# The first block's last norm as one combined sum with the recurrent layer's norm, and recurrent operands in PSUM

## The chip, the cores and the metric

The kernel runs on one core of a Trainium2 chip. The metric is the device time of one execution in microseconds (us), the median of several runs. Engines: TensorE (PE) with its weight load (PEld), VectorE (DVE), ScalarE (ACT), GpSimd (POOL), SyncE (SP, here only DMA issues).

## What is computed

A sequence of 512 tokens of width 1024 goes through a first block (modulated attention with a gated linear branch, then a convolutional feed-forward) and a second block of four layers, each a mixer and an MLP. Layers 0 and 3 have the recurrent mixer, layer 1 a spatial one, layer 2 a short convolution. What matters here, with `rms_norm(x, g) = x * rsqrt(mean(x*x) + EPS) * g` and EPS 1e-6:

```python
# end of the first block
x_lat = x_lat + gt2 * conv_ffn(h, ...)
return rms_norm(x_lat, final_g)

# start of the second block, layer 0 (recurrent) and layer 3 (recurrent)
h = _rmsnorm(x, norm_mix_g[i])
gate, xr = split(h @ w_in, 2)
gate = gelu(gate)
xr = causal_dwconv(xr, conv_w) + conv_b            # 4 taps
r  = sigmoid(block_diagonal(xr, gate_a_w) + gate_a_b)
ig = sigmoid(block_diagonal(xr, gate_x_w) + gate_x_b)
log_a = -8 * r * softplus(-lam)
a = exp(log_a)
u = sqrt(-expm1(2 * log_a)) * (ig * xr)
hs = scan(a, u)                                    # over time
x = x + (hs * gate) @ w_out
```

Two norms stand back to back where the blocks meet: the first block's last, of the sum x, and the recurrent layer's, of the normalised x. The normalised x is itself needed later, for the residual.

## The kernel before, in words

**Layout.** Everything is kept transposed: features on the 128 partitions, the 512 tokens along the free axis, so x is 8 tiles `x[:, k, :]` of 128x512 and a recurrent width of 1280 is 10 tiles. Each product is made in three parts for precision: an operand is split into a high and a low half (`h_hi`, `h_lo`; `rec_hi`, `rec_lo`), the weights too (`w_hi`, `w_lo`), and a tile of product is high by high, low by high, high by low (L1540 to L1551).

**Weights.** SP loads panels of 8 weight tiles into a ring of 4 slots, in order of use. GpSimd makes `w_hi` (L1473) and then `w_lo` (L1483) of each; it goes on when TensorE has begun with the panel that frees the slot. All are chained by semaphores (`panel_made`, `panel_used`).

**TensorE** writes outputs in a fixed order, output number o into bank o mod 4 of `acc` (4 PSUM banks); `begin_out` waits until the output four before has been taken. `stat` is a fifth bank, `side` three more. Norm sums are a product of `ones` with a sum of squares (L1583).

**The handover between the blocks.** VectorE adds each output of the last down projection to x (`gated_add`, L1350); ScalarE squares it (`sq`, L805); VectorE adds up the squares (`add_up`, L1069). When all 8 are in, TensorE sums over partitions (L1583), ScalarE takes the root (L815), VectorE the reciprocal (L1075) and rescales x by it and by `final1` (L1428). Each rescaled tile goes through `feed` and `feed_low`: square and high half on ScalarE (L1699, L1703), sum and `h_lo` on VectorE (L1885 or L1888, L1895). TensorE's first projection waits for `h_lo` tile by tile; its norm sum, root (L1709) and reciprocal (L1900) follow. The projections run on unnormalised h, and the outputs are rescaled by `rstd` afterwards.

**The recurrent layer** (functions `recurrent` on PE at L1588, on ACT at L1711, on DVE at L1915) has two halves of five tiles. TensorE makes five projections, then for each tile two gate products of two or three weight tiles each; a product for tile m needs neighbouring tiles of `rec_hi` and `rec_lo` (`BD`). After both halves come ten more projections (the y phase) and the down projection, whose first four outputs are made in two passes over the ten inputs (`down_in_two`).

VectorE's order is written out by hand: `convolved` rescales the bank (L1923), writes the bias into the first three columns (L1931, from `ones` in SBUF), and adds the four taps (L1936, two of L1939, and L1942, which writes into the bank). ScalarE (`conv_high`, L1719 and L1720) copies the bank to `rec_x` and to `rec_hi`; VectorE's `low` (L1948) makes `rec_lo` from the bank and sets the bank free. In the first half the order is convolved(m), low(m-1); in the second half the five ratios of the first half (L1963, on `rec_u` and `rec_sq`, both in SBUF) stand behind the first convolution. ScalarE's `decays` (L1730) makes tanh and two exponentials per tile, waiting for a ratio before it reuses one of the four tiles of `rec_sq`; `roots` (L1749) follow. In the y phase VectorE multiplies and scans the second half (`scanned`, L1966), and per output rescales the bank, multiplies it with the scan (`gated`, L1980) after ScalarE's gelu, and makes `y_low`. In the order before, y outputs 2 and on stand behind all five scans.

## Time and profile before

| | |
|---|---|
| median of 3 runs | 3293.4 us (3291.03 to 3296.08) |
| the profiled execution's own time | 3291.95 us |
| its span in the profile | 3290.2 us |
| mean granted TensorE clock | 0.972 of full speed |
| busy share PE, DVE, ACT, POOL | 95%, 46%, 21%, 57% |
| HBM traffic | 302.84 MB read, 93 GB/s over the span |

The profile is one execution taken by the hardware profiler. Its times are in us from the start of the span. The ends of the pipelined matmuls are modelled, so two starts in a row tell more than one duration. In a row such as `acc<-h_hi,w_hi` the output stands left of the arrow and the inputs right; the names in an overlay carry its prefix (`rec_rec_lo` is `rec_lo`). A row "A <- B" of the waits says that A's engine stood idle until B's instruction released it. A line number is that of the program text above.

The handover lies near 1086 to 1118 us, the first recurrent layer from there to about 1290, the second from about 2705 to 2890.

### The profile page before, as it was taken

The page shows a single profiled execution, that of the slowest core. Times are in us where ns is not written, and L with a number is a line of the kernel's source. Part 1 is how long each engine was busy: PE and PEld are TensorE (multiplying, and loading weights), DVE is VectorE, ACT ScalarE, POOL GpSimd, SP SyncE. Part 2 cuts the span into 40 slices and gives each one's busy share as a digit, 9 for nine tenths or more (in the row PEclk, how much of TensorE's full clock was granted, in tenths as well). Part 3 has the DMA queues.
Part 4 walks back from the last instruction along what each step waited for, and adds up shares of the span by engine and source line. Part 5 has one row for each costly group of instructions (what it writes and reads, how often), then busy time and mean ns, then how long its engine had stood idle before and what let it go on. Part 6 is the DMA issues. An engine that isn't in the chain of part 4 may idle for free.

```text
span 3290.2 us, 37587 instructions
## 1 busy us (share of the span) xinstructions
PE 3116.0 (95%) x13568; PEld 2492.1 (76%) x13568; DVE 1528.4 (46%) x1918; ACT 707.3 (21%) x1203; POOL 1876.1 (57%) x1030
## 2 busy tenths in 40 slices
PE   5878799989999799999999999999999998999998
PEld 3666646868888578888878888888888886888886
DVE  7876763247633774422236422266522247642222
ACT  3244463111100352200013211110211114421110
POOL 3412203646666466666666666666666665666664
PEclk8988899999999899999999999999999999999999
DMA  6601002222222122222222222222222222222221
GB/s 245 244 26 39 33 1 77 96 77 96 96 96 96 59 95 96 95 97 96 96 96 90 96 96 96 96 96 96 91 98 97 97 91 89 93 93 97 97 95 69
DMA packets 86009, 306.68 MB, mean 93 GB/s; under 512 B 9552, under 2 KB 10064, under 8 KB 85632
## 3 DMA queue, kind: packets, MB, share of 16 engines
q1 hardware_dynamic: 82512, 297.73, 26.6%
q10 hardware_dynamic: 3376, 7.24, 0.6%
q8 instruction: 87, 1.43, 0.2%
q14 instruction: 34, 0.28, 0.0%
HBM read 302.84 MB, written 2.10 MB: 93 GB/s over the span
## 4 chain that ended last, share of the span: by engine, by line
PE 83%; DVE 11%; ACT 2%; issue 2%; SPq 1%; DMA 1%; ACTq 0%; DVEq 0%
PE acc L1520 78%; PE side L727 1%; DVE rec_rec_x L1939 1%; DVE ada_more L1105 1%; PE acc L705 1%; DVE state L1251 1%; DMA xc<-in_ctx 1%; SPq L497 1%; DVE rec_rec_u L1963 0%; PE acc L631 0%; DVE acc L1942 0%; DVE rec_rec_x L1936 0%; DVE square_sum L1888 0%; DVE acc L1923 0%; DVE rec_rec_x L1931 0%
## 5 line engine op out<-in xcount | busy, mean ns | idle before, releaser
L1483 POOL TENSOR_TENSOR w_lo<-w_raw,w_hi 128x1024 fp32r<-128x1024 f32 x513 | 1243.6, 2424 | 1345.3 <-PE acc L1520 1298.9
L1520 PE MATMUL acc<-h_hi,w_hi 128*128 128x512 f32 x2224 | 881.6, 396 | 61.9 <-DVE state L1251 14.5
L1520 PE MATMUL acc<-h_hi,w_lo 128*128 128x512 f32 x2224 | 872.4, 392 | 0.0
L1520 PE MATMUL acc<-h_lo,w_hi 128*128 128x512 f32 x2224 | 872.4, 392 | 0.0
L1473 POOL TENSOR_SCALAR w_hi<-w_raw 128x1024 fp32r<-128x1024 f32 x513 | 650.1, 1267 | 37.3 <-DMA w_raw<-in_weights 37.3
L1520 PEld LDWEIGHTS acc<-h_hi,w_hi 128*128 128x128 f32 x2224 | 420.9, 189 | 170.1 <-issue 18.8
L1520 PEld LDWEIGHTS acc<-h_hi,w_lo 128*128 128x128 f32 x2224 | 421.3, 189 | 86.4
L1520 PEld LDWEIGHTS acc<-h_lo,w_hi 128*128 128x128 f32 x2224 | 421.6, 190 | 85.3 <-issue 1.7
L1906 DVE TENSOR_TENSOR x<-acc,x 128x512 f32 (+1 forms) x160 | 110.7, 692 | 635.5 <-PE acc L1520 635.3
L1520 PE MATMUL acc<-mlp_hid_hi,w_hi 128*128 128x512 f32 x1024 | 403.5, 394 | 0.0
L1520 PE MATMUL acc<-mlp_hid_hi,w_lo 128*128 128x512 f32 x1024 | 401.4, 392 | 0.0
L1520 PE MATMUL acc<-mlp_hid_lo,w_hi 128*128 128x512 f32 x1024 | 397.4, 388 | 0.0
L1834 ACT ACTIVATE mlp_hidden<-mlp_relu 128x512 f32<-128x512 f32 x128 | 81.0, 633 | 884.1 <-DVE mlp_relu L2115 884.1
L1913 DVE TENSOR_TENSOR mlp_hid_lo<-mlp_hidden,mlp_hid_hi 128x512 f32 (+1 forms) x128 | 157.4, 1230 | 177.5 <-ACT mlp_hid_hi L1835 177.5
L1520 PEld LDWEIGHTS acc<-mlp_hid_hi,w_lo 128*128 128x128 f32 x1024 | 192.2, 188 | 45.1
L1520 PEld LDWEIGHTS acc<-mlp_hid_lo,w_hi 128*128 128x128 f32 x1024 | 192.2, 188 | 43.0
L1520 PEld LDWEIGHTS acc<-mlp_hid_hi,w_hi 128*128 128x128 f32 x1024 | 192.5, 188 | 38.4
L2115 DVE SCALAR_TENSOR_TENSOR mlp_relu<-acc,rstd 128x512 f32<-128x512 f32 x128 | 88.6, 692 | 268.7 <-PE acc L1520 267.7
L1699 ACT ACTIVATE side<-x 128x512 f32<-128x512 f32 x72 | 43.4, 602 | 468.9 <-DVE x L1906 458.8
L1520 PE MATMUL acc<-rec_rec_hi,w_hi 128*128 128x512 f32 x264 | 107.8, 408 | 22.4 <-DVE rec_rec_lo L1948 22.4
L1383 DVE SCALAR_TENSOR_TENSOR ff_conv<-acc,table,ff_conv 128x441 f32<-128x441 f32 (+2 forms) x176 | 122.4, 695 | 6.3
L1520 PE MATMUL acc<-rec_rec_hi,w_lo 128*128 128x512 f32 x264 | 106.5, 403 | 0.0
(323 smaller groups left out, 3505.2 us busy)
## 6 DMA issues: line engine op xcount, KB each, us to landing
w_raw<-in_weights SPq DMA_DIRECT2D x513, 512.0 KB, 3.2
ada<-in_ada SPq DMA_DIRECT2D x36, 512.0 KB, 5.4
ada_more<-in_ada SPq DMA_DIRECT2D x10, 512.0 KB, 18.4
x<-in_x ACTq DMA_DIRECT2D x16, 256.0 KB, 6.6
out<-x SPq DMA_DIRECT2D x8, 256.0 KB, 2.2
cvec<-in_cvec ACTq DMA_DIRECT2D x1, 1024.0 KB, 5.8
ada_n<-in_ada SPq DMA_DIRECT2D x2, 512.0 KB, 17.5
xc<-in_ctx SPq DMA_DIRECT2D x1, 1024.0 KB, 16.9
```

What stands on the lines that cost most here:

```text
L497: sp.dma_start(ada_slot[slot], io["ada"][m]).then_inc(ada_in[slot], 16)
L705: pe.matmul(out[:, 0:c1 - c0], q_t[0:QK, h, P * qb:P * qb + P], k_t[0:QK, h, c0:c1], start=True, stop=True).then_inc(out_made, 1)
L727: ins = pe.matmul(side[rows, h % 2, :], v_mla[:, b, 64 * h:64 * h + 64], p_t[:, b, :], start=(b == 0), stop=(b == KB - 1))
L1383: ins = dve.scalar_tensor_tensor(out=out, in0=src[:, r0 + r:r1 + r, c0 + c:c1 + c], scalar=col("conv_w", FF1 * tap + j), in1=out, op0=ALU. ...
L1473: pool.tensor_scalar(w_hi[:, slot, :], w_raw[:, slot, :], 1.0, 1.0, ALU.mult, ALU.mult).then_inc(hi_made, 1)
L1483: pool.tensor_tensor(w_lo[:, slot, :], w_raw[:, slot, :], w_hi[:, slot, :].bitcast(F32), ALU.subtract).then_inc(panel_made, 1)
L1520: ins = pe.matmul(out, lhs, rhs, start=start, stop=stop, skip_group_check=group)
L1699: act.activation(squares(norm, k), x[:, k, :], ACT.Square).then_inc(squared, 1)
L1834: act.activation(M["hidden"][:, o % 4, :], M["relu"][:, o % 4, :], ACT.Square)
L1906: dve.tensor_tensor(tile, bank(o), tile, ALU.add).then_inc(out_taken[o % BANKS], 1)
L1913: dve.tensor_tensor(lo, whole_, hi.bitcast(F32), ALU.subtract).then_inc(made_sem, 1)
L2115: dve.scalar_tensor_tensor(out=M["relu"][:, o % 4, :], in0=bank(o), scalar=0.0, in1=rstd[:, :], op0=ALU.max, op1=ALU.mult).then_inc(out_ta ...
```

## The change

1. The first block's last norm is no longer made ahead of the recurrent layer. `FIRST_NORMS` goes from 4 to 3, `norm_sum(3)` is gone. Behind each `gated_add` ScalarE makes two squares, of x times `final1` and of x alone, and the high half of x times the product of both gains (`gain2[:, KT:]`); VectorE (`both_sums`) adds up the first squares, adds EPS times the second ones to it, keeps a sum of the second ones alone, and makes `h_lo` directly from x. The combined root uses `eps_eps`, EPS squared.
2. x itself is normalised later: TensorE makes a second sum product behind the norm's (L1583 stays), ScalarE its root, and VectorE (`first_norm`) a reciprocal and eight rescalings of x, inside the y phase's loop of the first recurrent layer.
3. `convolved` accumulates all four taps in `rec_x`, the newest tap first over all 512 columns, and the bias operation on three columns is gone. `conv_high` copies `rec_x` back into the bank and makes `rec_hi` from `rec_x`.
4. The exponential that the ratio reads goes to PSUM (`side` and `stat`) for four of five tiles, and ScalarE's wait for a ratio is gone. In the second half ratios 3 and 4 stand behind the second convolution.
5. In the y phase outputs 2 and 3 are moved in between the scans, and from output 4 on the bank of the next output is rescaled, not that of the one after.

```diff
-FIRST_NORMS = 4
+FIRST_NORMS = 3
...
-rec_a=([P, RT, T], F32), rec_u=([P, HALF, T], F32), rec_sq=([P, 4, T], F32))
+rec_a=([P, RT, T], F32), rec_u=([P, HALF, T], F32), rec_sq=([P, T], F32))
...
+        def decay_square():
+            return scan_input()[0:4] + [M["rec_sq"][:, :]]
...
             down(2)
-            norm_sum(3)
...
             for k in range(KT):
                 wait_taken(act, o + k)
-                sq(k, 3, x)
-            root_of(3)
-            for k in range(KT):
-                feed(k, NORM0, ("norm_mix", 0), lambda k: act.wait_ge(x_normed, k + 1), o)
+                act.wait_ge(summed, KT * NORM0 + k - 1)
+                act.activation(spare_bank[k % 2], x[:, k, :], ACT.Square, scale=col("final1", k)).then_inc(squared, 1)
+                if k:
+                    act.wait_ge(own_summed, k)
+                act.activation(side[:, 0, :], x[:, k, :], ACT.Square).then_inc(own_squared, 1)
...
+                act.activation(h_hi[:, k, :], x[:, k, :], ACT.Copy, scale=gain2[:, KT + k:KT + k + 1]).then_inc(h_hi_made, 1)
...
+            def both_sums(k):
+                scaled_sum, own_sum, own_square = square_sum[:, :], square[:, 0, :], side[:, 0, :]
+                dve.wait_ge(squared, KT * NORM0 + k + 1)
...
+                    link(dve.tensor_tensor(scaled_sum, spare_bank[k % 2], scaled_sum, ALU.add))
+                dve.wait_ge(own_squared, k + 1)
+                own(dve.scalar_tensor_tensor(out=scaled_sum, in0=own_square, scalar=EPS, in1=scaled_sum, op0=ALU.mult, op1=ALU.add),
+                    summed, KT * NORM0 + k + 1)
...
+                    own(dve.tensor_tensor(own_sum, own_square, own_sum, ALU.add), own_summed, k + 1)
+                dve.wait_ge(h_hi_made, KT * NORM0 + k + 1)
+                dve.scalar_tensor_tensor(out=h_lo[:, k, :], in0=x[:, k, :], scalar=gain2[:, KT + k:KT + k + 1],
+                                         in1=h_hi[:, k, :].bitcast(F32), op0=ALU.mult, op1=ALU.subtract).then_inc(h_lo_made, 1)
...
                             norm_sum(norm)
+                            if inst == 0:
+                                pe.wait_ge(own_summed, KT)
+                                pe.matmul(side[:, 0, :], ones[:, :], square[:, 0, :], start=True, stop=True).then_inc(own_stat, 1)
...
-                    act.activation(M["rec_x"][:, m, :], bank(o), ACT.Copy)
-                    act.activation(M["rec_hi"][:, m, :], bank(o), ACT.Copy).then_inc(rec_hi_made, 1)
+                    act.activation(bank(o), M["rec_x"][:, m, :], ACT.Copy)
+                    act.activation(M["rec_hi"][:, m, :], M["rec_x"][:, m, :], ACT.Copy).then_inc(rec_hi_made, 1)
...
-                            if i >= 4:
-                                act.wait_ge(rec_ratio, done + i - 3)
...
-                            act.activation(M["rec_sq"][:, i % 4, :], a, ACT.Exp, scale=rec_cl[:, 0, m:m + 1]).then_inc(rec_tanh, 1)
+                            act.activation(decay_square()[i], a, ACT.Exp, scale=rec_cl[:, 0, m:m + 1]).then_inc(rec_tanh, 1)
...
+                if inst == 0:
+                    act.wait_ge(own_stat, 1)
+                    act.activation(square[:, 1, :], side[:, 0, :], ACT.Sqrt, bias=col("eps"), scale=1.0 / D).then_inc(own_root, 1)
+                    act.wait_ge(own_root, 1)
...
-                    dve.tensor_scalar(acc_[:, 0:A_TAPS - 1], ones[:, 0:A_TAPS - 1], col("a_conv_b", first + m), None, ALU.mult)
-                    for j in range(A_TAPS - 1):
...
+                    for back in range(A_TAPS):
+                        tap = w[A_TAPS - 1 - back]
+                        dve.wait_ge(rec_tap, n0 + back + 1)
+                        if back == 0:
+                            dve.tensor_scalar(acc_, xr, tap, col("a_conv_b", first + m), ALU.mult, ALU.add).then_inc(rec_tap, 1)
+                        else:
+                            dve.scalar_tensor_tensor(out=acc_[:, back:], in0=xr[:, 0:T - back], scalar=tap, in1=acc_[:, back:],
+                                                     op0=ALU.mult, op1=ALU.add)\
+                               .then_inc(rec_conv if back == A_TAPS - 1 else rec_tap, 1)
...
+                def first_norm(i):
+                    if i == 0:
+                        dve.wait_ge(own_root, 1)
+                        dve.reciprocal(square[:, 1, :], square[:, 1, :]).then_inc(own_rstd, 1)
+                        dve.wait_ge(own_rstd, 1)
+                    for k in range(2 * i - 2, 2 * i):
+                        if 0 <= k < KT:
+                            dve.scalar_tensor_tensor(out=x[:, k, :], in0=x[:, k, :], scalar=col("final1", k), in1=square[:, 1, :],
+                                                     op0=ALU.mult, op1=ALU.mult).then_inc(x_normed, 1)
...
                 convolved(o, HALF)
-                for i in range(HALF):
+                for i in range(3):
                     ratio(first, i)
                 conv_low(o, HALF)
+                convolved(o + 1, HALF + 1)
+                for i in range(3, HALF):
+                    ratio(first, i)
+                conv_low(o + 1, HALF + 1)
...
-                for i in range(2, HALF):
-                    scanned(first + HALF, i, gates[1])
-                for m in range(2, RT):
+                scanned(first + HALF, 2, gates[1])
+                gated(o + 2, 2)
+                scanned(first + HALF, 3, gates[1])
+                y_low(o + 2, 2)
+                scaled_bank(o + 4, rec_gated)
+                gated(o + 3, 3)
+                scanned(first + HALF, 4, gates[1])
+                y_low(o + 3, 3)
+                for m in range(4, RT):
+                    if m + 1 < RT:
+                        scaled_bank(o + m + 1, rec_gated)
                     gated(o + m, m)
-                    if m + 2 < RT:
-                        scaled_bank(o + m + 2, rec_gated)
                     y_low(o + m, m)
+                    if inst == 0:
+                        first_norm(m - 4)
```

## Rows read from the trace of the kernel before

**Rows 1.** The page, busy time of each engine, whole span.

```profile
PE 3116.0 (95%) x13568; PEld 2492.1 (76%) x13568; DVE 1528.4 (46%) x1918; ACT 707.3 (21%) x1203; POOL 1876.1 (57%) x1030
```

**Rows 2.** TensorE's waits, whole span: who for, us in total, times, longest.

```profile
PE acc L1520 <- DVE rec_rec_lo L1948: 26.2, 10, 3.8
...
PE acc L1520 <- DVE h_lo L1895: 11.7, 8, 7.1
```

**Rows 3.** Timeline of the handover: start, us, engine, operation, [idle before it <- releaser].

```profile
1083.28 1.05 POOL L1473 TENSOR_SCALAR w_hi<-w_raw 128x1024 fp32r<-128x1024 f32 x1
...
1086.09 0.75 DVE L1350 SCALAR_TENSOR_TENSOR x<-acc,mod,x 128x512 f32<-128x512 f32 x1 [2.73 <-PE acc L1520]
...
1091.25 3.36 DVE L1075 RECIPROCAL side<-root 128x512 f32<-128x512 f32 x1 [2.89 <-ACT root L815]
...
1098.55 2.35 POOL L1483 TENSOR_TENSOR w_lo<-w_raw,w_hi 128x1024 fp32r<-128x1024 f32 x1 [14.23 <-PE acc L1520]
...
1098.65 2.80 DVE L1895 SCALAR_TENSOR_TENSOR h_lo<-x,table,h_hi 128x512 fp32r<-128x512 f32 x1
...
1112.36 0.50 PE L1520 MATMUL acc<-h_hi,w_hi 128*128 128x512 f32 x1 [0.30 <-DVE h_lo L1895]
```

**Rows 4.** Waits in the recurrent layers: first layer three, second layer two.

```profile
1142.51 0.50 PE L1520 MATMUL acc<-rec_rec_hi,w_hi 128*128 128x512 f32 x1 [3.77 <-DVE rec_rec_lo L1948]
...
PE acc L1520 <- DVE rec_rec_lo L1948: 7.2, 3, 2.7
ACT rec_rec_u L1741 <- DVE rec_rec_u L1963: 5.5, 1, 5.5
...
PE acc L1520 <- DVE rec_rec_lo L1948: 1.9, 1, 1.9
...
PE acc L1520 <- DVE rec_rec_lo L1948: 3.8, 1, 3.8
...
PE acc L1520 <- DVE rec_rec_lo L1948: 7.6, 3, 2.8
```

**Rows 5.** VectorE's groups: busy us, mean ns; then L1895's ns min/median/max.

```profile
L1895 DVE SCALAR_TENSOR_TENSOR h_lo<-x,table,h_hi 128x512 fp32r<-128x512 f32 x64 | 102.8, 1606 | 0.0
...
L1963 DVE SCALAR_TENSOR_TENSOR rec_rec_u<-rec_rec_sq,rec_rec_u 128x512 f32<-128x512 f32 x20 | 32.5, 1665 | 6.5 <-ACT rec_rec_sq L1742 6.5
...
L1923 DVE TENSOR_TENSOR acc<-acc,rstd 128x512 f32<-128x512 f32 x40 | 27.6, 691 | 36.0 <-PE acc L1520 35.9
L1948 DVE TENSOR_TENSOR rec_rec_lo<-acc,rec_rec_hi 128x512 fp32r<-128x512 f32 x40 | 27.2, 684 | 5.3 <-ACT rec_rec_hi L1760 2.7 <-ACT rec_rec_hi L1720 2.3
...
L1936 DVE TENSOR_SCALAR rec_rec_x<-acc,table 128x509 f32<-128x509 f32 x20 | 16.0, 799 | 0.0
L1931 DVE TENSOR_SCALAR rec_rec_x<-ones,table 128x3 f32<-128x3 f32 x20 | 15.6, 781 | 0.0
...
L1939 DVE SCALAR_TENSOR_TENSOR rec_rec_x<-acc,table,rec_rec_x 128x511 f32<-128x511 f32 x20 | 15.0, 750 | 0.7
...
L1895 DVE SCALAR_TENSOR_TENSOR h_lo<-x,table,h_hi x64: 737/2109/2802, 1096.7 to 2927.3; 128x512 fp32r<-128x512 f32 x64
```

**Rows 6.** The chain that ended last: start, us, what.

```profile
1142.51 22.44 PE acc L1520 x90
...
1197.61 17.00 PE acc L1520 x66
...
1332.89 344.61 PE acc L1520 x1512
...
2738.76 23.25 PE acc L1520 x90
...
2794.73 17.15 PE acc L1520 x66
```

**Rows 7.** The y phase: VectorE's wait; busy (x), PEclk, DMA share, GB/s.

```profile
DVE acc L1923 <- PE acc L1520: 13.9, 4, 3.5
...
1246.00:1272.00 26.00, 24.05 (x106) 19.60 (x105) 11.98 (x19) 6.50 (x11) 14.17 (x10) 1.00 0.28 100
```

More of the change, by code:

```diff
@@ L294, in build @@
         PE_NORMS = 0 if start_x else 2
-        H_SKIP = 0 if start_x else KT
+        H_SKIP = 0
         def bank(o):
@@ L461, in build @@
         x_normed = sem("x_normed")
+        own_squared = sem("own_squared")
+        own_summed = sem("own_summed")
+        own_stat = sem("own_stat")
+        own_root = sem("own_root")
+        own_rstd = sem("own_rstd")
         def sums(norm):
@@ L1035, in first_block_act @@
                 wait_taken(act, o + k)
-                sq(k, 3, x)
-            root_of(3)
-            for k in range(KT):
-                feed(k, NORM0, ("norm_mix", 0), lambda k: act.wait_ge(x_normed, k + 1), o)
+                act.wait_ge(summed, KT * NORM0 + k - 1)
[3 more added lines that the diff above has]
+                act.activation(side[:, 0, :], x[:, k, :], ACT.Square).then_inc(own_squared, 1)
+                if k == 0:
+                    act.wait_ge(gains_made, 4)
+                    wait_made(act, o - 1)
+                act.activation(h_hi[:, k, :], x[:, k, :], ACT.Copy, scale=gain2[:, KT + k:KT + k + 1]).then_inc(h_hi_made, 1)
         last_of = [slice(CHUNK - 1, CHUNK), slice(0, 1)]
@@ L1153, in first_block_dve @@
                 gains_made, 3)
+            own(dve.tensor_tensor(gain2[:, KT:2 * KT], table[:, names["final1"]:names["final1"] + KT],
+                                  table[:, names["norm_mix"]:names["norm_mix"] + KT], ALU.mult), gains_made, 4)
             dve.wait_ge(side_made, 1)
@@ L1411, in up @@
                 hidden_low(group, n - 1)
+            def both_sums(k):
+                scaled_sum, own_sum, own_square = square_sum[:, :], square[:, 0, :], side[:, 0, :]
+                dve.wait_ge(squared, KT * NORM0 + k + 1)
+                if k == 0:
+                    dve.wait_ge(stat_made, NORM0 - PE_NORMS)
+                    link(dve.tensor_copy(scaled_sum, spare_bank[k % 2]))
+                else:
[3 more added lines that the diff above has]
+                    summed, KT * NORM0 + k + 1)
+                if k == 0:
+                    own(dve.tensor_copy(own_sum, own_square), own_summed, 1)
+                else:
+                    own(dve.tensor_tensor(own_sum, own_square, own_sum, ALU.add), own_summed, k + 1)
+                dve.wait_ge(h_hi_made, KT * NORM0 + k + 1)
+                dve.scalar_tensor_tensor(out=h_lo[:, k, :], in0=x[:, k, :], scalar=gain2[:, KT + k:KT + k + 1],
+                                         in1=h_hi[:, k, :].bitcast(F32), op0=ALU.mult, op1=ALU.subtract).then_inc(h_lo_made, 1)
             up(0)
@@ L1423, in first_block_dve @@
                 if k:
-                    add_up(k - 1, 3)
-            rstd_of(3)
-            for k in range(KT + 1):
-                if k < KT:
-                    dve.scalar_tensor_tensor(out=x[:, k, :], in0=x[:, k, :], scalar=col("final1", k), in1=side[:, 0, :],
-                                             op0=ALU.mult, op1=ALU.mult).then_inc(x_normed, 1)
-                if k:
-                    dve.wait_ge(x_normed, k)
-                    feed(k - 1, NORM0)
-                    feed_low(k - 1, NORM0, ("norm_mix", 0))
+                    both_sums(k - 1)
         def load_panel(eng, slot, panel):
@@ L1708, in norm_root @@
                     act.wait_ge(rstd_made, norm)
-                act.activation(root[:, :], stat[:, :], ACT.Sqrt, bias=col("eps"), scale=1.0 / D).then_inc(root_made, 1)
+                act.activation(root[:, :], stat[:, :], ACT.Sqrt, bias=col("eps_eps" if norm == NORM0 else "eps"), scale=1.0 / D)\
+                   .then_inc(root_made, 1)
             def recurrent(inst, layer, norm):
@@ L1962, in ratio @@
                     dve.wait_ge(rec_tanh, 2 * (done + i + 1))
[L1963 removed]
+                    dve.scalar_tensor_tensor(out=M["rec_u"][:, i, :], in0=decay_square()[i], scalar=1.0,
                                              in1=M["rec_u"][:, i, :], op0=ALU.add, op1=ALU.mult).then_inc(rec_ratio, 1)
@@ L1995, in recurrent @@
                 convolved(o, HALF)
-                for i in range(HALF):
+                for i in range(3):
                     ratio(first, i)
                 conv_low(o, HALF)
-                for i in range(1, HALF + 1):
+                convolved(o + 1, HALF + 1)
+                for i in range(3, HALF):
+                    ratio(first, i)
+                conv_low(o + 1, HALF + 1)
+                for i in range(2, HALF + 1):
                     if i < HALF:
                         convolved(o + i, HALF + i)
-                    if i > 1:
+                    if i > 2:
                         conv_low(o + i - 1, HALF + i - 1)
@@ L2272, in second_table @@
         "b_norm_g": features(g["b_norm_g_2"]), "c_conv_w": features(g["c_conv_w_2"]),
-        "eps": np.full((P, 1), EPS, np.float32), "one": np.ones((P, 1), np.float32),
+        "eps": np.full((P, 1), EPS, np.float32), "eps_eps": np.full((P, 1), EPS * EPS, np.float32), "one": np.ones((P, 1), np.float32),
     }
```

13 lines of the change are left out of this document (2 added, 11 removed).

## The prediction

> **What bounds the kernel now.** I read the page first: TensorE is busy 95% of the span, VectorE 46%, ScalarE 21%, GpSimd 57% [rows 1]. So a gain can only come from moments in which TensorE stands still or runs at its lower clock, and the next view is who TensorE waits for. Of its waits over the whole span, two belong to lines of this diff: 26.2 us in 10 waits for `rec_lo` (L1948, the low half of an operand of the recurrent layers) and 11.7 us in 8 waits for `h_lo` (L1895) [rows 2]. The timeline then shows the second wait in place. VectorE adds the last tile to x at 1086.09; a sum, a product, a root, a 3.36 us reciprocal and eight rescaled tiles follow one after the other, and the last of the eight tile products of the next projection starts only at 1112.36 [rows 3].
>
> The first wait is spread over both recurrent layers: 3.77 us before the second block of gates, 7.2 us in 3 waits at the second half, 1.9 us in the y phase; in the other recurrent layer 3.8, 7.6 and (same pattern) 1.9 [rows 4]. What is late there is always VectorE's chain: rescale, four taps, low half, tile after tile. The groups show why. A 3-column operation (L1931) takes 781 ns on average, and the ratio (L1963) 1665 ns, and the 64 `h_lo` operations (L1895, both inputs in SBUF) take anything from 737 to 2802 ns; operations with a PSUM operand average 684 to 799 ns [rows 5]. In the handover one `h_lo` took 2.80 us: it started at 1098.65, 0.1 us behind GpSimd's 2.35 us subtraction [rows 3]. So VectorE operations that read only SBUF queue behind GpSimd's.
>
> **Part 1, the first block's last norm.** Removed: PE sum, root, reciprocal, eight rescalings and the second pass over the squares between the last add and the next projection. Added per tile: one more square on ScalarE and, on VectorE, a combining operation and a second sum. New end of the chain: the last add ends at 1086.84. Then tiles 6 and 7 each need two sums at about 0.68, one combining operation at 0.75 and an `h_lo` at 0.74, 2.9 us together; two tiles give 1092.7. ScalarE's three operations per tile (0.6, 0.6, 0.7) fit inside. TensorE may start tiles 0 to 5 at once, reaches tile 7 at 1091 and waits to 1092.7. Against 1112.36 that is **19.6 us earlier**, and the root follows at the same distance as before, so the reciprocal moves with it. Added on the path: the own sum's product, 0.9 us (estimate: a full-precision product is two passes of 0.43 us in the timeline; its root waits behind the main one and holds up nothing). If GpSimd is in the way of the three last `h_lo`, each costs up to 2.06 more (2.80 less 0.74); GpSimd's conversion of a panel ends at 1084.3 [rows 3], before tile 5's, and the next can't start before TensorE's first product at 1086, which leaves tile 7's free; so I take nothing, and keep 0 to 6 for the range.
>
> **Part 2, the convolution.** A tile now costs one rescaling 0.69, one first tap 0.80 and three taps at 0.75, less 0.1 of overlap where nothing waits: 3.8, plus 0.6 for a `low`. L1931 goes, 15.6 us for 20 tiles [rows 5]. VectorE is then ready for the fifth tile 17.0 us after the reciprocal (four tiles and three `low`), and TensorE, four projections of 5.47 us after the start of its second, delivers it some 17 to 18 us after it. So the new bound is that delivery: the second gate block needs the bank of tile 3, whose `low` stands behind the whole convolution of tile 4, 3.8 + 0.7 = 4.5 us after TensorE ends that tile; TensorE has 2.75 us of gate products meanwhile (four tiles at 0.684, from 344.61 us for 1512 products [rows 6]). The wait is 1.8 instead of 3.8: **2.0 gained**, once in each layer. That ScalarE now writes the bank back and reads SBUF for the high half changes its two operations by under 0.1 us, and only the last one of a half is waited for.
>
> **Part 3, the ratios.** Four of five ratios get a PSUM operand: 0.75 instead of 1.67, and two of the five move behind the next tile. Second half: from 1165.0, convolution of tile 5 (3.8), three ratios, `low` when ScalarE has finished its exponentials (its 5.5 us wait for a ratio [rows 4] is gone), about 1172.5. VectorE then catches up with TensorE, whose last projection ends four times 5.47 later, at 1187, and the wait is again the 1.8 us of part 2. The three old waits are 7.2 and 7.6 behind modelled ends, and 7.9 and 8.2 from start to start (0.2 more each), so **6.1 and 6.4 gained**. The fifth ratio stays in SBUF: 0 to 2.2 us each, taken as 0.
>
> **Clock.** After those waits TensorE's granted clock fell to its lower level for some products: 90 products took 22.44 and 23.25 us and 66 took 17.00 and 17.15 [rows 6], where full speed (2.4 GHz, 0.228 us each) gives 20.8 and 15.3 with the first fill. After the 1.9 us wait of the y phase the clock stayed at 1.00 [rows 7]. With 1.8 us waits only, I take back all of it: **3.3 us and 4.3 us**.
>
> **Part 4, the y phase.** y_low(2) no longer stands behind three scans but behind one; it is ready near 1244.5, before TensorE wants it (17.00 from 1197.61 [rows 6] and six projections: 1247.4), so **1.8** is gained in each layer. New in the first layer: a reciprocal of 3.35 and eight rescalings of x with both tensors in SBUF, at 1.61 each (the mean of L1895, the same kind of operation, mostly beside a working GpSimd [rows 5]), 16.2 us on VectorE. VectorE waited 13.9 us for TensorE in this stretch [rows 7]; what is over lands on the last two `low`, whose banks TensorE wants: **2.3 lost**. At 0.74 each nothing is lost, at 2.80 each 11.9 are.
>
> The rows say that such an operation costs 0.74 at its shortest and 1.61 on average [rows 5]. The Trainium skill (SBUF — State Buffer, on the shared port pair) says that a VectorE operation with two SBUF inputs and a GpSimd operation that reads SBUF exclude each other for a whole instruction. By that rule alone each of the eight could meet the 2.4 us subtraction and end 3.1 us after its start, which would make the loss 14 us instead of 2.3; the 2.80 maximum agrees with its size.
>
> **Sum.** First layer: 19.6 − 0.9 + 2.0 + 6.1 + 3.3 + 1.8 − 2.3 = 29.6. Second: 2.0 + 6.4 + 4.3 + 1.8 = 14.5. Together 44.1. The profiled execution took 3291.95, 1.4 under the median of 3293.4; taken from the median: **3249 us**. No DMA is moved: SP's panel requests follow GpSimd's conversions, which follow TensorE, and GpSimd is 57% busy, so weights are not late.
>
> **Rivals.**
> 1. *The port is dearer than its mean.* x rescaled at 2.80 (9.6 more), the three `h_lo` (6), the fifth ratios (4): up to 3269, half of it 3259. For it: the median of the 64 `h_lo` is 2.11 [rows 5], above the mean I use. Against: VectorE and GpSimd both pause between operations. Chance 0.15.
> 2. *The clock does not come back.* The 1.8 us waits stay, and if they still lower the clock, 7.6 of the sum are lost: 3257. Against: the y-phase row. Chance 0.12.
> 3. *The diff does less than it says.* ScalarE becomes what VectorE waits for in its place (the write-back to PSUM before the high half), and only part 1 pays: 3293.4 − 18.7 = 3275. Against: ScalarE is 21% busy. Chance 0.05.
> 4. *Slower.* The deferred rescaling of x in the y loop: beyond 13.9 us of slack each of its microseconds stops TensorE. It cancels all else when 3.35 + 8s − 13.9 exceeds 46.4 (the sum without its loss), s = 7.1 us; slower by 6.6 us (3300) needs 7.9. The longest operation of this kind was 2.80. Chance 0.03, and 0.02 for an end within 0.2%.
> 5. *More than forecast*, the 1.8 us waits gone too: 3242. Chance 0.05.
>
> The forecast has 0.58. **Range** 3240 to 3264: down to case 5, up through case 2 and half of case 1. A measurement of this kernel can tell about 0.2% (6.6 us) from no change; cases 1, 2, 3, 5 and the forecast are all faster by more: 0.95 faster, 0.02 same, 0.03 slower.
>
> **What would show it.** TensorE's waits for `rec_lo` fall from 26.2 to about 7 us in four waits, those for `h_lo` in the handover from 11.7 to about 2; no group of L1931's kind; ratios at 0.75 but two or four near 1.5; 0.228 us per product behind the gates' waits; in the y phase of the first layer a TensorE wait of 0 to 4 us before the down products. I am wrong in part 1 if tile 7's product starts more than 9 us after the last add, in parts 2 and 3 if the waits for `rec_lo` stay above 15 us, in part 4 if the down products of the first layer wait over 5 us.

## The result, and the profile after

The changed kernel takes **3256.86 us** (median of 4 runs, 3255.03 to 3257.22) against 3292.22 us before on the same chip (4 runs): a ratio of 0.9888, 95% interval 0.9876 to 0.99. The forecast was 3249 with a range of 3240 to 3264. The profiled span fell from 3290.2 to 3255.4, so 34.8 us of the 44.1 forecast came.

TensorE makes the same 13568 products as before [rows 1]. It stood idle 148.7 us of the span, against 174.2 before, and its busy time is 9.3 us shorter:

```profile
PE 3106.7 (95%) x13568; PEld 2489.8 (76%) x13568; DVE 1509.9 (46%) x1907; ACT 709.0 (22%) x1203; POOL 1875.7 (58%) x1030
```

Who TensorE waits for, whole span. The line that took 26.2 us in 10 waits [rows 2] now takes this, and the `h_lo` of the handover 3.9 us where the prediction said about 2:

```profile
PE acc L1545 <- DVE rec_rec_lo L1975: 9.1, 4, 2.7
...
PE acc L1545 <- DVE h_lo L1444: 3.9, 2, 2.7
```

The chain that ended last (start, us, what), beside [rows 6]:

```profile
727.53 342.18 PE acc L1545 x1494
...
1127.22 16.98 PE acc L1545 x66
...
1177.15 126.36 PE acc L1545 x546
...
1310.19 344.61 PE acc L1545 x1512
...
2713.95 17.02 PE acc L1545 x66
...
2763.92 124.77 PE acc L1545 x546
...
2895.37 344.61 PE acc L1545 x1512
```

The same view of the kernel before, in two rows that [rows 6] left out:

```profile
727.09 358.98 PE acc L1520 x1566
...
2930.10 344.61 PE acc L1520 x1512
```

These rows give a ruler that all the traces below share. The piece that begins at 727.53 (727.09 before) is the last long run of products ahead of the handover. It begins anywhere from 722.4 to 729.1 in the 14 traces of this study, and in two traces of one and the same kernel (run 9) at 727.53 and 723.04. So a profile's span carries several us that say nothing of the edit, and I compare three stretches instead: **A**, from this piece to the next one of 1512 products (the handover and the first recurrent layer), **B**, from there to the piece of 1512 products behind the other recurrent layer (2895.37), and their sum. Before, A is 605.80 and B 1597.21, together 2203.01; after, 582.66 and 1585.18, together 2167.84. **A gained 23.1 where 29.6 were forecast, B 12.0 where 14.5 were.**

The handover, VectorE's timeline with one row of GpSimd (start, us, engine, line, operation, what it waited for), beside [rows 3]. The add of a tile stands ahead of the sums and the `h_lo` of the tile before it, so the `h_lo` of 1081.53 is that of the fifth tile:

```profile
1076.94 1.72 DVE L1444 SCALAR_TENSOR_TENSOR h_lo<-x,gain,h_hi 128x512 fp32r<-128x512 f32 x1
...
1078.58 0.74 DVE L1364 SCALAR_TENSOR_TENSOR x<-acc,mod,x 128x512 f32<-128x512 f32 x1
...
1081.36 2.40 POOL L1508 TENSOR_TENSOR w_lo<-w_raw,w_hi 128x1024 fp32r<-128x1024 f32 x1 [1.79 <-PE acc L1545]
...
1081.53 2.77 DVE L1444 SCALAR_TENSOR_TENSOR h_lo<-x,gain,h_hi 128x512 fp32r<-128x512 f32 x1
1084.23 0.74 DVE L1364 SCALAR_TENSOR_TENSOR x<-acc,mod,x 128x512 f32<-128x512 f32 x1
1085.00 0.69 DVE L1435 TENSOR_TENSOR square_sum<-side,square_sum 128x512 f32<-128x512 f32 x1
1085.73 0.69 DVE L1437 SCALAR_TENSOR_TENSOR square_sum<-side,square_sum 128x512 f32<-128x512 f32 x1
1086.46 0.69 DVE L1442 TENSOR_TENSOR square<-side,square 128x512 f32<-128x512 f32 x1
1087.18 2.66 DVE L1444 SCALAR_TENSOR_TENSOR h_lo<-x,gain,h_hi 128x512 fp32r<-128x512 f32 x1
1089.77 0.74 DVE L1364 SCALAR_TENSOR_TENSOR x<-acc,mod,x 128x512 f32<-128x512 f32 x1
...
1095.55 0.75 DVE L1444 SCALAR_TENSOR_TENSOR h_lo<-x,gain,h_hi 128x512 fp32r<-128x512 f32 x1
```

The bracket with PE as the releaser, which the last add had before, is gone: VectorE goes from one operation into the next and is itself the bound. The last add stands 362.24 us behind the start of the long piece; before, it stood 359.00 behind it. TensorE then takes the eighth tile 6.59 us later, then the two row sums, then the next projection:

```profile
1096.36 0.80 PE L1545 MATMUL acc<-h_hi,w_hi 128*128 128x512 f32 x1 [1.19 <-DVE h_lo L1444]
...
1097.81 1.91 PE L1608 MATMUL stat<-square_sum,ones 128*128 128x512 f32 x2
1099.51 1.32 PE L1621 MATMUL side<-square,ones 128*128 128x512 f32 x2
1100.26 0.80 PE L1545 MATMUL acc<-h_hi,w_hi 128*128 128x512 f32 x1
```

The window over it (stretch and its length; busy us and count of PE, PEld, DVE, ACT, POOL; granted clock; DMA share, GB/s), and the first product of the same projection before:

```profile
1096.30:1101.00 4.70, 4.64 (x9) 2.65 (x10) 0.53 (x2) 0.82 (x2) 0.00 (x0) 0.60 0.00 0
```

```profile
1113.62 0.80 PE L1520 MATMUL acc<-h_hi,w_hi 128*128 128x512 f32 x1
```

The granted clock is 0.60 here, so most of the stretch ran at the lower of its two levels (1.2 GHz), behind two waits of 2.66 and 1.19 us for `h_lo`. From the eighth tile's product to the next projection are 3.90 us; in run 7 below, at a clock of 1.00 throughout, they are 2.12. After the change that projection's first product stands 372.73 behind the start of the long piece, against 386.53 before: the handover gained 13.8.

### The profile page after: what moved, and what is told of

Same layout as the page of the kernel before. It is cut to its first block, busy times and chain, and to the rows that moved or that the text cites. A ratio compares the mean times of both kernels' runs of the same rounds, so it can differ in the third digit from the quotient of the medians.

```text
span 3255.4 us, 37573 instructions
## 1 busy us (share of the span) xinstructions
PE 3106.7 (95%) x13568; PEld 2489.8 (76%) x13568; DVE 1509.9 (46%) x1907; ACT 709.0 (22%) x1203; POOL 1875.7 (58%) x1030
## 4 chain that ended last, share of the span: by engine, by line
PE 87%; DVE 9%; ACT 2%; issue 1%; SPq 1%; DMA 1%; ACTq 0%; DVEq 0%
PE acc L1545 81%; PE side L735 1%; DVE ada_more L1117 1%; DVE rec_rec_x L1968 1%; PE acc L713 1%; DVE state L1265 1%; DMA xc<-in_ctx 1%; SPq L505 1%; PE acc L639 0%; PE acc L621 0%; PE acc L606 0%; PE side L1545 0%; PE side L723 0%; DVE prob L1327 0%; PE stat L1608 0%
## 6 DMA issues: line engine op xcount, KB each, us to landing
xc<-in_ctx SPq DMA_DIRECT2D x1, 1024.0 KB, 16.8
```

## The experiments

Medians are of 4 or 5 runs. The ratio is to the kernel before, timed again beside each set: it took 3293.32 us beside runs 1 to 4, 3291.19 beside 5 to 8 and 3293.64 beside 9 to 12. The changed kernel itself took 3256.86 in one set and 3253.37 in another, so a difference of 3 us between two medians of different sets says nothing.

| kernel | median us | ratio, 95% interval | A | B | A + B |
|---|---|---|---|---|---|
| before | 3292.22 | 1 | 605.80 | 1597.21 | 2203.01 |
| changed | 3256.86 | 0.9888, 0.9876 to 0.99 | 582.66 | 1585.18 | 2167.84 |
| changed again (9) | 3253.37 | 0.9886, 0.9869 to 0.9902 | 581.82 | 1585.12 | 2166.94 |
| fold alone (1) | 3281.42 | 0.9966, 0.9952 to 0.9979 | 595.47 | 1597.41 | 2192.88 |
| recurrent edits alone (2) | 3267.06 | 0.992, 0.9906 to 0.9933 | 593.30 | 1583.44 | 2176.74 |
| ratio's operands in SBUF (3) | 3262.35 | 0.9906, 0.989 to 0.9921 | 582.61 | 1588.30 | 2170.91 |
| old convolution (4) | 3266.78 | 0.992, 0.9906 to 0.9933 | 583.43 | 1589.43 | 2172.86 |
| x not rescaled (5) | 3255.86 | 0.9891, 0.9876 to 0.9906 | 581.80 | 1585.24 | 2167.04 |
| old y order (6) | 3267.27 | 0.992, 0.9907 to 0.9934 | 588.55 | 1591.79 | 2180.34 |
| sums joined once (7) | 3250.36 | 0.9866, 0.985 to 0.9881 | 573.40 | 1586.36 | 2159.76 |
| `h_lo` first (8) | 3256.12 | 0.9886, 0.9871 to 0.9901 | 582.20 | 1585.44 | 2167.64 |
| early `low` (10) | 3257.56 | 0.9895, 0.9879 to 0.9912 | 580.98 | 1586.80 | 2167.78 |
| 7 and 10 (11) | 3252.24 | 0.9878, 0.9861 to 0.9894 | 576.37 | 1585.39 | 2161.76 |
| 7 and 8 (12) | 3250.17 | 0.9875, 0.9858 to 0.9891 | 576.31 | 1583.41 | 2159.72 |

**1. The fold alone.** The first block's edits, with the old convolution, ratios and orders:

```diff
-                    for back in range(A_TAPS):
+                    dve.tensor_scalar(acc_[:, 0:A_TAPS - 1], ones[:, 0:A_TAPS - 1], col("a_conv_b", first + m), None, ALU.mult)
...
-                            act.activation(decay_square()[i], a, ACT.Exp, scale=rec_cl[:, 0, m:m + 1]).then_inc(rec_tanh, 1)
+                            act.activation(M["rec_sq"][:, i % 4, :], a, ACT.Exp, scale=rec_cl[:, 0, m:m + 1]).then_inc(rec_tanh, 1)
```

> The kernel before with the fold of the first block's last norm alone (both_sums, the doubled statistic, the deferred rescaling of x); the recurrent layers keep the old convolution, the wait of the ratios, and the old order. Theory A (the parts add up, and the handover gave 13.8 us net in the trace of the changed kernel, while most of the rest came from the recurrent layers): 13 to 16 us under the kernel before, some 3277 us. Theory B (the fold alone makes nearly all of it, and the recurrent edits mostly shift waits): 25 us or more under before, 3267 us or less. As forecast by part 1 of the prediction: 18.7 us under before, 3274 us. The y phase keeps its old order here, in which x's rescaling may stall the first layer's output product: up to 4 us less gain under any theory.

Measured: 11.9 us less in the median, A shorter by 10.3, B unchanged. **2. The recurrent edits alone**, on the kernel before (the same two places the other way round, the new orders, no `both_sums`, no `first_norm`):

> The kernel before with all the edits of the recurrent layers and without the fold. Theory A: the two layers gained 34.8 less 13.8 us, so 19 to 22 us under the kernel before, some 3272 us, in two nearly equal halves (the second layer 12 us, the first 8 to 9). Theory B (mostly shifted waits): under 12 us of gain. The prediction's own terms for these parts sum to about 26.5 us without the deferred rescaling.

Measured: 26.3 us less, A shorter by 12.5, B by 13.8. The two gains of A + B, 10.1 and 26.3, add up to 36.4, where both together gave 35.2 and 36.1. So the recurrent edits carry nearly three quarters. That the sums agree is in part luck: run 1 has a stall of the y phase that the changed kernel has not (below), and run 2 has not the changed kernel's losses of clock, and the two nearly cancel. Theory B falls in both runs; in run 2 theory A was too low as well, and the prediction's own terms were nearest (13.2 and 14.5, together 27.7; the expectation had added them up to 26.5). The fold came short of its 13 to 16, as the expectation had allowed, because the old y order lets the rescaling of x stall TensorE. In the y phase of run 1, from the chain (two rescalings at a time):

```profile
1253.63 3.61 DVE x L2023 x2
...
1264.51 3.61 DVE x L2023 x2
...
1270.14 44.93 PE acc L1545 x195
```

From 1234.17, the first product behind the y phase's old wait, to 1321.74 are 87.57 us; before it was 83.68 from 1249.21. Of these 3.9 us some 1.4 are clock: behind the 1.95 us wait at 1234.17 the first 72 products took 18.22 us at a granted clock of 0.91, and 16.8 would be full speed. The rest, 2.4, is the stall, 1.76 of it one new wait for `rec_lo` at 1270.14. The handover as such gave 14.2: the first half's gates start 401.2 us behind the long piece, against 415.4 before.

**3. The ratio's operands back in SBUF**, and with them ScalarE's wait for a ratio. The order of the second half stays new.

```diff
-                    dve.scalar_tensor_tensor(out=M["rec_u"][:, i, :], in0=decay_square()[i], scalar=1.0,
+                    dve.scalar_tensor_tensor(out=M["rec_u"][:, i, :], in0=M["rec_sq"][:, i % 4, :], scalar=1.0,
```

> The changed kernel with the exponentials of the decay ratio back in SBUF (four tiles), so that a product of two bfloat16 or float32 SBUF tiles waits for the port pair again as before, the order of the second half unchanged. Theory A (each second half was bound by VectorE, and the ratios' operands in PSUM took the ratio off the contended port): 4 to 6 us slower per layer, 8 to 12 us over the changed kernel, 3265 to 3269 us. Theory B (the gain of the second half came from the order and the merged convolution, the ratio hides): within 2 us of the changed kernel.

Measured: 5.5 us slower than the changed kernel in the median, 3.1 to 4.0 in A + B, between both theories. TensorE's waits for `rec_lo`, and the ratios of one tile (ns min/median/max) in this kernel and in the changed one:

```profile
PE acc L1545 <- DVE rec_rec_lo L1977: 11.9, 6, 2.8
...
L1992 DVE SCALAR_TENSOR_TENSOR rec_rec_u<-rec_rec_sq,rec_rec_u x20: 678/928/2905, 1153.3 to 2799.3; 128x512 f32<-128x512 f32 x20
```

```profile
L1990 DVE SCALAR_TENSOR_TENSOR rec_rec_u<-side,rec_rec_u x12: 682/688/692, 1153.5 to 2789.2; 128x512 f32<-128x512 f32 x12
...
L1990 DVE SCALAR_TENSOR_TENSOR rec_rec_u<-rec_rec_sq,rec_rec_u x4: 691/1474/2261, 1161.6 to 2793.0; 128x512 f32<-128x512 f32 x4
```

With a PSUM operand all ratios take 0.68 to 0.69 us; with SBUF ones 0.68 to 2.9. The two new waits are 1.38 and 1.39 us, one per layer. The operand's place is thus 1.4 of the 6 us per layer in part 3, in waits. That the rest is the order and the shorter convolution follows by subtraction; no run has the old order alone.

**4. The old convolution.**

```diff
+                    dve.tensor_scalar(acc_[:, 0:A_TAPS - 1], ones[:, 0:A_TAPS - 1], col("a_conv_b", first + m), None, ALU.mult)
...
-                    act.activation(bank(o), M["rec_x"][:, m, :], ACT.Copy)
+                    act.activation(M["rec_x"][:, m, :], bank(o), ACT.Copy)
```

> The changed kernel with the old convolution (its bias added by a separate operation over three columns, and ScalarE's old part of the work). Theory A (the first half waits at its end for VectorE's last convolution, 1.8 us instead of 3.8): 2.0 us per first half and as much or somewhat more per second half, so 6 to 10 us over the changed kernel, 3263 to 3267 us. Theory B (the first half is bound by TensorE and only the second by VectorE, so a longer convolution is hidden in the first): 2 to 5 us over, 3259 to 3262 us.

Measured: 9.9 us slower in the median (theory A), 5.0 to 5.9 in A + B, of which 5.5 are waits for `rec_lo` (14.6 in 6 against 9.1 in 4); the profiled execution is the fastest of its five (3257.07, the others 3263.87 to 3268.68), so the trace understates it and I don't explain the rest. The gate waits at the end of the first halves are 3.78 and 3.82 us, the old ones [rows 4], against 1.82 in the changed kernel, where VectorE now stands idle 0.94 us for TensorE's bank ahead of the last convolution (1122.67). **Part 2's 2.0 us per layer is shown, and its reason too: TensorE's delivery is the bound.**

**5. x not rescaled** (the reciprocal and the eight products are left out). **6. The old y order.**

```diff
-                    if inst == 0:
-                        first_norm(m - 4)
```

> The changed kernel without the deferred rescaling of x (its reciprocal and its eight products on VectorE are left out, so the residual the block adds to is not rescaled; the time is read, not the values). The prediction charged the rescaling with 2.3 us of TensorE's wait in the first layer. Theory A (no charge, since in the changed kernel's trace TensorE never waits for it and the y phase runs through): within 2 us of the changed kernel, and the same 124.8 to 126.4 us behind the last gate wait. Theory B (the rescaling takes VectorE away when the second half's end still needs it): 2 to 4 us faster.

```diff
-                scanned(first + HALF, 2, gates[1])
-                gated(o + 2, 2)
...
+                for i in range(2, HALF):
+                    scanned(first + HALF, i, gates[1])
```

> The changed kernel with the old order of the y phase. Theory A (the old order held TensorE up once in each layer, 1.9 us, and the rescaling now stands in front of the pieces that TensorE wants): 3.8 us more at least, and up to 8 us more if the rescaling in the first layer stalls, so 3261 to 3265 us. The kernel with the fold alone, which has the old order, shows three pairs of rescalings in its chain of waits, so the upper part of this is the likelier. Theory B (the y order is worth nothing, TensorE is behind anyway): within 2 us of the changed kernel.

Without the rescaling A is 581.80, with it 582.66 and 581.82: it costs nothing (theory A). The comparison with run 9 (581.82) is the clean one, since the clock behind the two gate waits of A is the same in both (15.42 and 127.52 us here, 15.39 and 127.56 there). With the old y order the rescaling does cost time. TensorE's waits in the window 1215 to 1300 of run 6:

```profile
PE acc L1545 <- DVE rec_rec_lo L1975: 3.7, 2, 1.9
```

The changed kernel has none there. The median is 10.4 us above the changed kernel, more than the 4 to 8 expected: 5.6 us are added waits (14.7 in 7 against 9.1 in 4). Of the rest I can name clock: behind its four gate waits 66 products took 15.42, 18.48, 17.23 and 17.23 us, where 15.4 is full speed, and behind the first y wait of each layer the granted clock was 0.91.

**7. The two sums joined once, at the last tile**, so that VectorE has one operation less per tile:

```diff
-                own(dve.scalar_tensor_tensor(out=scaled_sum, in0=own_square, scalar=EPS, in1=scaled_sum, op0=ALU.mult, op1=ALU.add),
-                    summed, KT * NORM0 + k + 1)
...
+                if k == KT - 1:
+                    own(dve.scalar_tensor_tensor(out=scaled_sum, in0=own_sum, scalar=EPS, in1=scaled_sum, op0=ALU.mult, op1=ALU.add),
+                        summed, KT * NORM0 + KT)
```

> The changed kernel with the two sums of squares joined once, at the last tile, instead of at every tile (seven VectorE operations of 0.70 us fewer). Theory A (at the handover VectorE is late only behind the last residual add, where one joint of two lies on the path, tiles 6 and 7): 0.7 us to 1.4 us faster, near 3256 us. Theory B (the whole handover of VectorE, 13 us of back-to-back sums, is its own bound, so each of the joints of the last four tiles counts): 2.5 to 3.5 us faster, 3253 to 3254 us. Theory C (the wait goes to the split of the activations, h_lo, which the port holds up for 2.7 us at tiles 4 and 5): no gain, within 1 us.

Measured: 3250.36, the sum of stretches 7.2 to 8.1 shorter. By the traces all three theories were too low. The medians are weaker evidence: they give 6.5 against the changed kernel's first set and 3.0 against its second, which theory B covers, and the intervals of the ratios overlap (0.985 to 0.9881 against 0.9869 to 0.9902). What is shown is the gain at the handover, in the trace. Its timeline:

```profile
1077.44 2.47 DVE L1446 SCALAR_TENSOR_TENSOR h_lo<-x,gain,h_hi 128x512 fp32r<-128x512 f32 x1
...
1079.83 0.74 DVE L1364 SCALAR_TENSOR_TENSOR x<-acc,mod,x 128x512 f32<-128x512 f32 x1
...
1083.60 0.75 DVE L1364 SCALAR_TENSOR_TENSOR x<-acc,mod,x 128x512 f32<-128x512 f32 x1 [0.79 <-PE acc L1550]
1085.84 0.79 DVE L1446 SCALAR_TENSOR_TENSOR h_lo<-x,gain,h_hi 128x512 fp32r<-128x512 f32 x1
1087.80 0.75 DVE L1364 SCALAR_TENSOR_TENSOR x<-acc,mod,x 128x512 f32<-128x512 f32 x1 [1.17 <-PE acc L1550]
```

The adds wait for TensorE again, which gives one every 4.20 us (1083.60 to 1087.80). VectorE's own work per tile is now five operations less one: a single long `h_lo` (2.47) is made good one tile later. In the changed kernel it is 3.7 us with a short `h_lo` (five operations of 0.74), so only 0.5 per tile is free, and three long ones in a row (1.72, 2.77 and 2.66) push the last add back by 3.24. The last add is at 358.99 again, the next projection's first product at 366.59: **19.9 us earlier than before, where part 1 forecast 18.7**. These 6.1 us against the changed kernel are 3.2 of adds on time, 1.1 from the last add to the eighth tile's product (5.48 against 6.59, one joint fewer between them), and 1.8 of clock behind it. The rest of A's gain is clock behind the gates' waits (15.41 and 124.79 us, against 16.98 and 126.36).

**8. `h_lo` ahead of the sums.**

```diff
+                dve.wait_ge(h_hi_made, KT * NORM0 + k + 1)
+                dve.scalar_tensor_tensor(out=h_lo[:, k, :], in0=x[:, k, :], scalar=gain2[:, KT + k:KT + k + 1],
...
                 dve.wait_ge(squared, KT * NORM0 + k + 1)
```

> The changed kernel with ScalarE making h_hi before its two squares and VectorE making h_lo before its sums, tile by tile. Theory A (TensorE waits for h_lo, which stands last in each tile's work, and then for the sums, which it needs only at the end of the eighth tile): the product of tile 7 starts 2.1 us earlier behind the last residual add, the two row sums right behind it wait for the sums instead, so 0 to 1.5 us faster in the end, and the clock may hold. Theory B (the clock falls at this place because TensorE waits in pieces; filling them keeps it up): 2 to 4 us faster, and the row sums take 0.86 and 0.6 us instead of 1.71 and 1.11.

No gain (582.20). The product of the eighth tile does start 2.2 us sooner behind the last add, as theory A said (4.43 against 6.59), but the add itself comes later. Right behind the add, `h_lo` meets GpSimd's subtraction at four tiles in a row (2.46, 2.72, 2.79 and 2.67 us), and the adds come up to 5.7 us apart. One of the four:

```profile
1073.42 0.75 DVE L1364 SCALAR_TENSOR_TENSOR x<-acc,mod,x 128x512 f32<-128x512 f32 x1
...
1073.98 2.39 POOL L1508 TENSOR_TENSOR w_lo<-w_raw,w_hi 128x1024 fp32r<-128x1024 f32 x1 [1.74 <-PE acc L1545]
...
1074.20 2.72 DVE L1431 SCALAR_TENSOR_TENSOR h_lo<-x,gain,h_hi 128x512 fp32r<-128x512 f32 x1
...
1079.01 0.75 DVE L1364 SCALAR_TENSOR_TENSOR x<-acc,mod,x 128x512 f32<-128x512 f32 x1
```

The last add stands at 364.41, 2.2 later than in the changed kernel, which uses that up; the next projection starts at 372.57 (372.73 in the changed kernel).

**9. The changed kernel again**, with no edit.

> The changed kernel once more, unaltered, for a second trace of the same instructions. Theory A (what the clock does behind a gate wait is decided by the moment, not by the kernel: waits of 1.82 and 2.73 us of the same lines kept 1.00 in the kernel with the recurrent edits alone and fell to 0.90 in three of four cases in the changed kernel): the four waits are again 1.82, 2.73, 1.82 and 2.74 us, but the 66 products behind them take 15.4 or 17.0 us in another pattern than before, and the runs spread over 3 to 7 us. Theory B (the length of the wait and the work ahead of it decide): the same pattern, low, low, low, full. VectorE's adds of the handover lag TensorE by the same 2 us under both. Median 3257 us.

Measured: 3253.37. The add is at 362.23 and the waits are 1.81, 2.75, 1.82 and 2.72 us; the pattern of the clock is another at the first place (theory A). The two traces' windows behind the first gate wait, first this one, then the changed kernel's:

```profile
1122.30:1137.60 15.30, 15.30 (x67) 12.58 (x68) 3.46 (x5) 7.71 (x11) 7.75 (x5) 1.00 0.28 97
```

```profile
1127.20:1144.20 17.00, 16.98 (x67) 13.84 (x68) 3.46 (x5) 7.82 (x12) 7.85 (x5) 0.90 0.26 88
```

**10. The fourth tile's `low` ahead of the last convolution**; **11.** this with 7; **12.** 7 with 8.

```diff
+                conv_low(o + HALF - 2, HALF - 2)
+                convolved(o + HALF - 1, HALF - 1)
+                conv_low(o + HALF - 1, HALF - 1)
```

> The changed kernel with the low part of the fourth convolved tile made ahead of the last convolution of each half instead of behind it. Theory A (TensorE waits for the low part of the last tile, and VectorE's chain is the bound): 0.6 us less for each of the four waits, which become 1.2 and 2.1 us, so 2 to 3 us faster, plus up to 1.6 us for each place at which the clock then stays up. Theory B (the fourth tile's low part is what TensorE would run into next, so the moved operation delays the last one by as much): no change, within 1.5 us.

> The changed kernel with both: the two sums joined once at the last tile, and the low part ahead of the last convolution. Theory A (the two sit on different stretches of TensorE's chain and add up): the kernel with the single joint was at 0.9866 of the kernel before, so 1 to 3 us less than that, 3247 to 3250 us. Theory B (the moved low part brings nothing): at the single joint's time, 3250 us.

> The changed kernel with the single joint and with h_hi and h_lo made ahead of the sums. In the traces, the split h_lo made at once behind the residual add ran into GpSimd's split of the weights at every tile (2.46 to 2.79 us), and made behind two sums it met it at one tile of the last four. Theory A (VectorE's work per tile, with the port's delay in it, against the 4.2 to 5.6 us that TensorE gives it, decides the handover): 0.75 + 2.7 + 0.7 + 0.7 = 4.9 us a tile is more than TensorE's own pace at the faster tiles, so the last add is 1 to 2 us later behind TensorE than with the single joint alone, and the end is 0 to 2 us slower than with the single joint, 3250 to 3252 us. Theory B (only the order at the last tile counts): 1 to 2 us faster than the single joint, 3248 us.

Run 10 brings nothing. The gates of the first halves wait 1.34 and 1.70 instead of 1.82 and those of the second halves 3.29 instead of 2.73, since the moved `low` finds ScalarE's copies not made. VectorE's timeline of run 10:

```profile
1120.20 0.69 DVE L1975 TENSOR_TENSOR rec_rec_lo<-acc,rec_rec_hi 128x512 fp32r<-128x512 f32 x1 [0.62 <-ACT rec_rec_hi L1749]
...
1125.91 0.69 DVE L1975 TENSOR_TENSOR rec_rec_lo<-acc,rec_rec_hi 128x512 fp32r<-128x512 f32 x1 [1.22 <-ACT rec_rec_hi L1749]
```

In the old place the last convolution ran on VectorE while ScalarE made its copies, so the `low` behind it did not have to wait. Neither theory had this. Run 11 is at run 7's time or above (theory B). Run 12's median lies in theory A's range and the reason fails: the last add is not late (359.08); the row sum waits 1.09 us for its operand instead, and the projection starts 1.4 later than in run 7 (367.96). Its total is the same as run 7's only because it lost 1.6 us of clock behind its gate waits (17.00 for 66 products) where run 7 lost 2.8 (127.55 for 546). Run 7 is the version to keep: the smallest edit, and none was faster beyond the spread.

## Why the prediction was right, and by how much it was not

The forecast case happened in kind: every part gained, and 3256.86 lies in the range. What the prediction had not seen is that VectorE becomes the bound of the handover. The 8.9 us that are missing in A + B (44.1 less 35.2) fall on named terms.

- **Part 1, 18.7 forecast, 13.8 measured: 4.9 short.** The failed step is the sentence "I take nothing, and keep 0 to 6 for the range". I looked at the port only for the `h_lo` behind the last add. It acted earlier: the `h_lo` of the fourth, fifth and sixth tile took 1.72, 2.77 and 2.66, and the last add came 3.24 late. I had left the last add where it was, as though VectorE's three new operations per tile had room; they had 0.5 us. The test that I had set (over 9 us from last add to the eighth tile's product) did not fire, at 6.59; the time went ahead of it. The other 1.7 of the 4.9 are clock: the prediction has 2.2 us from the eighth tile's product to the next projection, and at a granted clock of 0.60 it took 3.90. Run 7 shows both, with one joint for eight and 19.9 gained. It changes two things at once, VectorE's work per tile and how many `h_lo` meet GpSimd, so it doesn't say how much either alone would give.
- **Own sum's product, 0.9.** At full clock it adds 0.86 (run 7). In the changed kernel it fell into the slow stretch that part 1's 1.7 us already holds.
- **Part 2, 2.0 per layer.** Right in size and reason: waits of 1.82, and 3.78 and 3.82 with the old convolution.
- **Part 3, 6.1 and 6.4.** 0.9 short in each layer: the second gates wait 2.73 and 2.74, not 1.8. The `low` of the sixth tile waited for ScalarE until 1156.61, which is where the forecast had it (done near 1172.5, less the 15.3 us by which the second half starts earlier). From there VectorE runs without a gap through the last convolution, so what was put too low lies behind it: the fifth ratio, in SBUF, took 2.26 in each layer instead of 0.68, where I had taken 0 of a possible 2.2. These 1.6 us are more than the 0.9 that are missing. This is worked out from the trace; no run varies that ratio alone.
- **Clock, 3.3 and 4.3 forecast.** "I take back all of it" failed: rival 2 in large part. Three of four places stayed low (16.98 and 17.02 for 66 products against 15.39; 126.36 for 546 against 124.77), so 3.2 of 3.3 in the first layer and 1.6 of 4.3 in the second did not come. The step rested on one row, the 1.9 us wait of the y phase with 1.00 behind it [rows 7]; the same wait in run 1 was followed by 0.91. In run 2, with the same waits, no place was low, and its gains were 12.5 and 13.8 where the prediction's terms without the fold are 13.2 and 14.5. So these parts together are near their size there; that a 1.8 us wait keeps the clock up is not so in general.
- **Part 4, y order 1.8, rescaling 2.3 lost.** The first is shown by run 6, whose second layer has one wait of 1.9 us more, and not the second: run 5 without it is no faster. The eight took 1.05 us on average, not 1.61, so the work was 11.7 us and stayed below the 13.9 us of slack.

```profile
L2017 DVE SCALAR_TENSOR_TENSOR x<-x,table,square 128x512 f32<-128x512 f32 x8 | 8.0, 1046 | 0.0
```

From the rule of the Trainium skill (SBUF — State Buffer, on the shared port pair) the prediction had worked out a bound of 14 us for this. The trace bears out what the page says of the single meeting (2.77 beside a 2.40 us subtraction), and each of the eight does not meet one. In the old y order of run 6 the same eight took 1.82 each: the moment at which they are issued sets how many meet.

In sum 4.9 + 3.2 + 1.6 + 1.8 fell short and 2.3 was not lost: 9.2, against the 8.9 that are missing. So rival 2 came true in large part, and rival 1 in two of its three places (the `h_lo` and the fifth ratios) but not in the third, the rescaling of x. How near the number came is in part luck: some 6.5 us of what fell short are clock, which differs between executions of one kernel, and the 2.3 that were charged for nothing offset a part of it.

## What to carry to other kernels

Work that is folded into a stage of another engine must be held against that stage's pace per tile, with the contended duration of each operation and not its shortest: here VectorE had 4.20 us per tile, and 3.7 plus two port delays of 2 us was too much, while 3.0 plus one was not. An operation that can be done once behind such a loop should leave it: here one joint instead of eight gave 6 us at the handover, where moving `h_lo` within the loop gave nothing. And compare kernels that differ by a few us by a stretch between two events of the trace, since what lies ahead of the first one alone differed by 4.5 us between two traces of one kernel.

## What the runs showed of the hardware that I had not expected

The same instructions with the same 1.82 us wait went on at full clock in one execution (15.39 us for 66 products) and at 0.90 of it in another (16.98). Where it fell, 1.6 to 3.1 us were lost (127.56 for 546 products in run 9 is 2.8; 18.48 for 66 in run 6 is 3.1). Over the nine traces with a first gate wait of 1.8 us, full speed followed in the first layer in runs 2, 3, 5, 6, 7, 8 and 9, and not in the changed kernel's first trace and in run 12. In the other recurrent layer the same wait was followed by full speed only in runs 2, 7 and 12. A gain that rests on the clock has therefore to be given as a chance. What decides it at such a wait, the runs don't tell.

An operation with two SBUF inputs that met GpSimd's subtraction did not merely run slower: each of the long `h_lo` ended 0.54 to 0.56 us behind the end of the subtraction, however early it had started (1084.30 behind 1083.76 for the fifth tile; 1.07 us long in run 7 where it had started late, 2.72 in run 8 where it had started early). So it is long or short by the moment. In a loop without gaps it can fall into step with GpSimd and be long at tile after tile (run 8), and the single joint of run 7 broke the step.
